# Moving the fourth weight unit's low part to GpSimd and the second residual tile to VectorE at the borders of a decoder trunk

## The chip, the cores and the metric

The kernel runs on one core of a Trainium2 chip. The metric is the device time of one execution in microseconds. A run is the time of one execution; the numbers below are the median of three runs, and one more execution that was profiled.

## The reference

The reference is a decoder trunk of four layers over 272 tokens (16 learned ones and 256 of the input) with 1024 features, in float32. Every layer has three sub-layers, and each is wrapped in two norms:

```
h = h + 0.5 * rmsnorm(swiglu_1(rmsnorm(h, g0)), g1)
h = h +       rmsnorm(mixer   (rmsnorm(h, g2)), g3)
h = h + 0.5 * rmsnorm(swiglu_2(rmsnorm(h, g4)), g5)
```

`rmsnorm(x, g)` is `x * rsqrt(mean(x*x) + eps) * g`. The mixers are stick-breaking attention (layers 0 and 3), latent attention with a rotary key (layer 1) and RWKV-7 time mixing (layer 2). A SwiGLU is `silu(h @ gate) * (h @ up)` times an output matrix, with 2816 hidden features.

## The kernel before

The activations lie with the features on the 128 partitions: `h`, `m`, `x_hi` and `x_lo` hold eight tiles of 128 features by 272 tokens each. A product in nearly full float32 precision is made of three passes of TensorE over numbers that are split in two: with `w = w_hi + w_lo` and `x = x_hi + x_lo` it adds `w_hi*x_hi`, `w_hi*x_lo` and `w_lo*x_hi` into one bank of PSUM.

The weights come in units of up to 1408 columns of 128 features, one after the other through a ring of four slots. SyncE loads a unit into `raw`, ScalarE copies it into `w_hi` (`split_hi`), and GpSimd subtracts `w_lo = raw - w_hi` in two halves (`split_lo`, line 1685). TensorE waits for `lo_ready` of a unit before it uses it, and SyncE waits for it before it loads the slot again. A run of units that belong to one matrix is a section. All engines have their own program, written out by hand in order, and they meet only at semaphores; the order of the work on an engine is the order of the code.

A **border** is the place where one sub-layer ends and the next begins. There are eleven of them inside the trunk, and what happens there is this:

- TensorE ends the output matrix, sums the squares of the output (lines 452 and 454) and runs some products that nobody reads (line 460).
- ScalarE makes the factor `rsqrt(mean + eps)` with two instructions (1193 and 1196) and writes it to bank 4 of PSUM.
- VectorE scales the eight tiles of the output, `m[k] = m[k] * gain * bank[4]` (line 1918, below "scale k"). Tile 0 it adds to the residual itself, `h[0] += m[0]` (line 1922). The call `steps.link` makes it wait for its own scale first.
- GpSimd adds the tiles 1 to 7, `h[k] += m[k]` (`add_residual`, line 1719), each as soon as VectorE has scaled it.
- ScalarE makes `x_hi[k] = h[k] * gain` (line 1227) as soon as tile k of `h` is there, and then its squares (1229).
- VectorE makes the low part `x_lo[k] = h[k] * gain - x_hi[k]` (line 1825, below "low k"). With `LAG = 3` low 0 stands behind scale 3 in its program, low 1 behind scale 4, and so on.
- TensorE begins the next section with `first_round` (line 384): for each tile k it waits for `x_hi[k]`, does the four products of the first two units that need only that (416 and 417), for odd k also three products of the third unit (400 to 402), then waits for `x_lo[k]` and does two more products (424). It goes to tile k + 1 only then. The next norm's own factor is not needed for this: it is applied to the results.
- Behind low 7 VectorE adds up the squares (1832 to 1834) for the sum that TensorE makes in line 382.

Three of the next section's first four units get their low part from GpSimd during the last round of the section before (`output_section`). The fourth one's is made by VectorE (line 1910), between the copy of the last output tile and scale 0. The border that leads to time mixing (its next section is called `lora1`) is apart: there GpSimd makes the fourth unit's low part behind the residual, in one instruction of 1024 columns. The border to latent attention uses the tiles through `product` (lines 339 to 341), which needs `x_hi` and `x_lo` at once.

Of the kernel before, what the change touches and what calls it, by code (L numbers as in the profile page):

```python
# [19 lines left out]
P = 128  # L20
D = 1024
DT_ = D // P
# [7 lines left out]
RING = 4  # L30
# [4 lines left out]
LAG = 3  # L35
SUM_AFTER = 6
FILL = 10
WARM = 12
NCH, LEVELS = 5, 6
PAIRS = 4  # L40
# [58 lines left out]
def build(nc, A, out, layers):  # L99
    secs = sections(plan_of(layers))  # L100
    ctx = ExitStack()
    with ctx:
# [4 lines left out]
        h = sb("h", [P, DT_, L])  # L107
        m = sb("m", [P, DT_, L])
        raw = sb("raw", [P, RING, CAP * P])
# [19 lines left out]
        bank = [ctx.enter_context(nc.psum_tensor(f"bank{b}", [P, 512], F32)) for b in range(8)]  # L129
# [3 lines left out]
        w_hi, w_lo = (xplace.enter_context(nc.sbuf_tensor(n, [P, RING, CAP * P], F32R)) for n in ("w_hi", "w_lo"))  # L133
# [89 lines left out]
        hi_ready, lo_ready = sem("hi_ready"), sem("lo_ready")  # L223
# [6 lines left out]
        apply_ready, h_ready = sem("apply_ready"), sem("h_ready")  # L230
# [31 lines left out]
        def rounds(eng, sec, body, ahead, peel=False):  # L262
# [6 lines left out]
                    body(i, lambda s: ahead(sec, i + 1, s))  # L269
            after = following[sec.name_key]  # L270
            body(sec.iters - 1, lambda s: ahead(after, 0, s) if after else None)

        def fourth_unit_by_vector(sec):

            return following[sec.name_key] is not None and following[sec.name_key].name != "lora1"

        def leads_to_mixing(sec):

            return following[sec.name_key] is not None and following[sec.name_key].name == "lora1"
# [10 lines left out]
        following = {s.name_key: t for s, t in zip(secs, secs[1:] + [None])}  # L290

        def gain(layer, sub, post, j):
            c = ((layer * 3 + sub) * 2 + post) * DT_ + j
            return gains[:, c:c + 1]
# [6 lines left out]
        def _(pe):  # L301
# [10 lines left out]
            def taken(*banks):  # L312
                for b in banks:
                    pe.wait_ge(bank_free[b], uses[b] + 1)
# [132 lines left out]
            def sum_output(after):  # L447
# [8 lines left out]
                if after is not None:  # L456
                    taken(7)
                    pe.wait_ge(cbf_ready, 1)
                    for _ in range(FILL):
                        nc.tensor.matmul(bank[7][:, :], ident_bf, cbf[:, 0:512], start=True, stop=True)  # L460
# [656 lines left out]
            taken(7)  # L1117
            for _ in range(WARM):
                nc.tensor.matmul(bank[7][:, 0:L], std[:, 0:P], std[:, :], start=True, stop=True)
# [554 lines left out]
        def _(pool):  # L1674
# [19 lines left out]
            def output_section():  # L1694


                sec = next(take)

                def body(i, ahead):
                    for s in range(RING):  # L1700
                        if not (following[sec.name_key] is not None and s == 3 and isinstance(i, int) and i == sec.iters - 1):
                            ahead(s)
                rounds(pool, sec, body, split_lo)
                if following[sec.name_key] is None:
                    for at, k in enumerate((1, 3, 5, 7)):
                        pool.wait_ge(apply_ready, n["apply"] + at + 1)
                        c = slice(n["cut"], L)
                        nc.gpsimd.tensor_tensor(h[:, k, c], h[:, k, c], m[:, k, c], ALU.add).then_inc(last_pool_ready, 1)
                else:
                    add_residual(sec)  # L1710
                if leads_to_mixing(sec):
                    split_lo(following[sec.name_key], 0, 3)

            def add_residual(sec):
                for k in range(1, DT_):
                    n["apply"] += 1
                    pool.wait_ge(apply_ready, n["apply"])
                    c = slice(n["cut"], L)
                    nc.gpsimd.tensor_tensor(h[:, k, c], h[:, k, c], m[:, k, c], ALU.add).then_inc(h_ready, 1)  # L1719
# [7 lines left out]
            def time_mixing():  # L1727
                for s in range(RING):
                    pool.wait_ge(lhi_ready, s + 1)
                    nc.gpsimd.tensor_tensor(lr_lo[:, s, :], lt[:, s, :], lr_hi[:, s, :], ALU.subtract).then_inc(lr_ready, 1)  # L1730
                for _ in range(5):
                    next(take)
                vec = lambda c: vecs[:, c:c + 1]

                def level_part(lv, p):

                    total = chunks_of(lv)
                    if lv > 1:
                        pool.wait_ge(y_done, core_at[("Y", lv - 1), p][3] + 2)
                    for s in (2 * p, 2 * p + 1):  # L1740
                        nc.gpsimd.tensor_tensor(chunks(aml[:, s, 0:TC * total]), chunks(am[:, s, 0:TC * total]), per_chunk(m_level[lv], total),
                                                ALU.mult).then_inc(aml_ready, 1)

                for p in range(PAIRS):
                    X, first, second, _ = core_at["A", p]
                    pool.wait_ge(bank_free[X], first + 1)
                    pool.wait_ge(bank_free[X + 1], second + 1)
                    pool.wait_ge(gram_done, core_at["Rb", p][3] + 2)
                    for s in (2 * p, 2 * p + 1):
                        nc.gpsimd.tensor_tensor(chunks(tinv[:, s, :]), chunks(am[:, s, :]), per_chunk(m_level[0], NCH),  # L1750
                                                ALU.mult).then_inc(level0_made, 1)
                    for s in (2 * p, 2 * p + 1):
                        pool.wait_ge(level0_made, s + 1)
                        nc.gpsimd.tensor_tensor(chunks(tinv[:, s, :]), chunks(tinv[:, s, :]), per_chunk(ident64, NCH),
                                                ALU.add).then_inc(tinv0_ready, 1)
                    level_part(1, p)
                    for k in (2 * p, 2 * p + 1):
                        pool.wait_ge(bank_free[k], uses_at["bonus"][k] + 2)
                        nc.gpsimd.tensor_scalar_add(m[:, k, :], m[:, k, :], vec(V_LNB + k)).then_inc(offset_made, 1)
                for lv in range(2, LEVELS):  # L1760
                    for p in range(PAIRS):
                        level_part(lv, p)
                for k in range(DT_):
                    pool.wait_ge(offset_made, k + 1)
                    nc.gpsimd.tensor_tensor(m[:, k, :], m[:, k, :], g_[:, k, :], ALU.mult).then_inc(offset_ready, 1)
                for k in range(DT_):
                    pool.wait_ge(offset_ready, k + 1)
                    nc.gpsimd.tensor_scalar_mul(g_[:, k, :], g_[:, k, :], vec(V_LNW + k)).then_inc(scaled_gate_ready, 1)
                pool.wait_ge(sa_done, 4 * NCH)
                sec_out = next(take)  # L1770
                for s in range(RING):
                    split_lo(sec_out, 0, s)
                low_parts(x_lo, x_hi, DT_)
                for s in range(RING):
                    split_lo(sec_out, 1, s)
                for s in range(3):
                    split_lo(following[sec_out.name_key], 0, s)
                add_residual(sec_out)

            pool.wait_ge(lo_ready, 2)  # L1780
# [29 lines left out]
        def _(dve):  # L1810
            steps = Steps(dve, dve_chain)
            n = dict(sq=0, sg=0, std=0, head=0, mhead=0, vt=0, xf=0, x=0, gained=0, hsq=0, kept=0, cut=0)
            cols = lambda: slice(n["cut"], L)
# [62 lines left out]
            def last_product(sec, layer, sub, then=None):  # L1876
# [25 lines left out]
                rounds(dve, sec, body, lambda *a: None)  # L1902
                n["sq"] += DT_
                n["kept"] += 1
                if fourth_unit_by_vector(sec):
                    after = following[sec.name_key]
                    w = slice(0, after.blocks * P)
                    dve.wait_ge(hi_ready, after.start + 4)
                    dve.wait_ge(lo_ready, after.start + 3)
                    nc.vector.tensor_tensor(w_lo[:, 3, w], raw[:, 3, w], w_hi[:, 3, w], ALU.subtract).then_inc(lo_ready, 1)  # L1910
                b = 2 if two else 3
                dve.wait_ge(bank_free[b], uses_at[sec.name_key][b] + sec.iters + 1)
                inverse_root()
# [1 line left out]
                    last_residual(layer, sub)  # L1915
                    return
                for k in range(DT_):
                    scaled = nc.vector.scalar_tensor_tensor(m[:, k, cols()], m[:, k, cols()], gain(layer, sub, 1, k), bank[4][:, cols()],  # L1918
                                                            ALU.mult, ALU.mult)
                    if k == 0:  # L1920
                        steps.link(scaled)
                        nc.vector.tensor_tensor(h[:, 0, cols()], h[:, 0, cols()], m[:, 0, cols()], ALU.add).then_inc(h_ready, 1)
                    else:
                        scaled.then_inc(apply_ready, 1)
                    if then and k >= LAG:
                        low_part(*then, k - LAG)
# [602 lines left out]
```

## Time and profile before

| | us |
|---|---|
| median of three runs | 2333.43 |
| lowest and highest | 2330.32, 2334.26 |
| the profiled execution | 2328.99 |
| its span, first to last instruction | 2327.2 |
| TensorE busy in the span | 2238.4 (96%) |
| GpSimd busy | 1701.5 (73%) |
| ScalarE busy | 1052.2 (45%) |
| VectorE busy | 906.4 (39%) |

The span is the time that the trace covers, and the profiled execution took 1.8 us more than it. A line of a timeline begins with the start of an instruction and how long it took, both in us; the brackets at its end tell how long the engine was idle before it, and what it then was released by. Matmuls overlap, so each is shown as longer than the distance to the next.

### The profile page before, as it was taken

What the parts mean: (1) busy time and instruction counts of PE and PEld (TensorE: products, weight loads), DVE (VectorE), ACT (ScalarE), POOL (GpSimd) and SP (SyncE); (2) the same over time, 40 slices, a digit from 0 to 9 for tenths busy, and PEclk for the clock granted to TensorE, in tenths of its full rate; (3) what the DMA queues carried; (4) which work ended last, traced back from release to release, by engine and by line L of the source; (5) the groups of instructions that cost most, each with busy time, mean ns of one, the idle gap of its engine ahead of it and who ended that gap; (6) DMA issues with size and microseconds to landing.
All of it is one profiled execution on the core that took longest, in us unless ns stands there. A gap on an engine that the chain in (4) does not pass through costs nothing. (4 is left out here: it accounts for less than half of the span.)

```text
span 2327.2 us, 54272 instructions
## 1 busy us (share of the span) xinstructions
PE 2238.4 (96%) x20693; PEld 2175.7 (93%) x20704; DVE 906.4 (39%) x1911; ACT 1052.2 (45%) x1545; POOL 1701.5 (73%) x1306
## 2 busy tenths in 40 slices
PE   9999999999999889999999898789999999999998
PEld 8999999999999879999999897679999999999997
DVE  4322334313331434322431987734322331344331
ACT  5444545444443545344444573335444434465442
POOL 6887758887887728887888403838887888766996
PEclk9999999999999999999999999999999999999999
DMA  6553544554554314563555242015554555433662
GB/s 217 171 196 126 158 127 152 173 199 128 179 192 146 127 46 154 171 199 127 181 185 180 99 157 68 3 39 163 174 197 134 172 179 188 141 126 127 191 206 99
DMA packets 90125, 348.82 MB, mean 150 GB/s; under 512 B 10016, under 2 KB 11808, under 8 KB 90016
## 3 DMA queue, kind: packets, MB, share of 16 engines
q1 hardware_dynamic: 90016, 347.31, 46.2%
q8 instruction: 75, 1.23, 0.2%
q14 instruction: 34, 0.28, 0.0%
HBM read 346.22 MB, written 1.05 MB: 149 GB/s over the span
## 5 line engine op out<-in xcount | busy, mean ns | idle before, releaser
L1685 POOL TENSOR_TENSOR w_lo<-raw,w_hi 128x512 fp32r<-128x512 f32 (+4 forms) x1124 | 1547.0, 1412 | 420.7 <-ACT w_hi L1182 401.2
L339 PE MATMUL bank<-x_hi,w_hi 128*128 128x272 f32 (+1 forms) x3264 | 946.3, 290 | 3.5 <-DVE x_lo L1825 1.9
L341 PE MATMUL bank<-x_hi,w_lo 128*128 128x272 f32 (+1 forms) x3264 | 942.2, 289 | 0.0
L340 PE MATMUL bank<-x_lo,w_hi 128*128 128x272 f32 (+1 forms) x3264 | 938.3, 287 | 0.0
L1182 ACT ACTIVATE w_hi<-raw 128x1024 fp32r<-128x1024 f32 (+2 forms) x608 | 678.7, 1119 | 386.4 <-PE bank L341 368.7
L339 PEld LDWEIGHTS bank<-x_hi,w_hi 128*128 128x128 f32 x3264 | 615.5, 189 | 7.0 <-DVE hid_lo L1963 3.1
L340 PEld LDWEIGHTS bank<-x_lo,w_hi 128*128 128x128 f32 x3264 | 616.1, 189 | 0.1
L341 PEld LDWEIGHTS bank<-x_hi,w_lo 128*128 128x128 f32 x3264 | 615.6, 189 | 0.0
L339 PE MATMUL bank<-hid_hi,w_hi 128*128 128x272 f32 (+1 forms) x1408 | 404.1, 287 | 0.0
L341 PE MATMUL bank<-hid_hi,w_lo 128*128 128x272 f32 (+1 forms) x1408 | 403.7, 287 | 0.0
L340 PE MATMUL bank<-hid_lo,w_hi 128*128 128x272 f32 (+1 forms) x1408 | 403.0, 286 | 0.0
L339 PEld LDWEIGHTS bank<-hid_hi,w_hi 128*128 128x128 f32 x1408 | 265.0, 188 | 0.0
L340 PEld LDWEIGHTS bank<-hid_lo,w_hi 128*128 128x128 f32 x1408 | 264.9, 188 | 0.0
L341 PEld LDWEIGHTS bank<-hid_hi,w_lo 128*128 128x128 f32 x1408 | 264.6, 188 | 0.0
L1286 ACT ACTIVATE sg<-gs 128x272 f32<-128x272 f32 (+1 forms) x176 | 75.6, 429 | 393.7 <-DVE gs L1844 393.7
L1895 DVE COPY m<-bank 128x272 f32 (+3 forms) x96 | 42.1, 439 | 523.1 <-ACT sq L1187 523.1
L1956 DVE TENSOR_TENSOR bank<-bank,xr 128x272 f32<-128x272 f32 (+1 forms) x176 | 78.6, 447 | 394.1 <-PE bank L341 394.1
L1187 ACT ACTIVATE sq<-bank 128x272 f32<-128x272 f32 (+1 forms) x96 | 38.0, 396 | 239.9 <-PE bank L341 233.1
L1844 DVE TENSOR_TENSOR gs<-bank,xr 128x272 f32<-128x272 f32 (+1 forms) x176 | 77.2, 439 | 161.7 <-PE bank L341 142.6
L1719 POOL TENSOR_TENSOR h<-h,m 128x272 f32<-128x272 f32 (+1 forms) x77 | 70.5, 949 | 40.0 <-DVE m L1918 40.0
L1961 DVE CAST hid_hi<-bank 128x272 f32 (+3 forms) x176 | 77.3, 439 | 24.6 <-DVE bank L1959 12.9
L1959 DVE TENSOR_TENSOR bank<-sg,bank 128x272 f32<-128x272 f32 (+1 forms) x176 | 78.1, 444 | 21.7 <-ACT sg L1286 16.2
(379 smaller groups left out, 2367.7 us busy)
## 6 DMA issues: line engine op xcount, KB each, us to landing
raw<-in_ffn_in SPq DMA_DIRECT2D x352, 512.0 KB, 3.5
raw<-in_ffn_out SPq DMA_DIRECT2D x128, 704.0 KB, 4.1
raw<-in_sb_in SPq DMA_DIRECT2D x48, 512.0 KB, 3.5
raw<-in_rw_in SPq DMA_DIRECT2D x24, 512.0 KB, 3.2
raw<-in_sb_out SPq DMA_DIRECT2D x16, 512.0 KB, 3.5
raw<-in_mla_out SPq DMA_DIRECT2D x8, 512.0 KB, 3.2
raw<-in_rw_lora SPq DMA_DIRECT2D x8, 512.0 KB, 3.2
raw<-in_rw_out SPq DMA_DIRECT2D x8, 512.0 KB, 4.0
```

What stands on the lines that cost most here:

```text
L339: nc.tensor.matmul(o, wh, xh[:, k, cols()], start=start, stop=False)
L340: nc.tensor.matmul(o, wh, xl[:, k, cols()], start=False, stop=False)
L341: last = nc.tensor.matmul(o, wl, xh[:, k, cols()], start=False, stop=stop)
L1182: nc.scalar.activation(w_hi[:, s, 0:sec.blocks * P], raw[:, s, 0:sec.blocks * P], ACT.Copy).then_inc(hi_ready, 1)
L1286: nc.scalar.activation(sg[:, f, cols()], gs[:, f, cols()], ACT.Silu).then_inc(sg_ready, 1)
L1685: part = nc.gpsimd.tensor_tensor(w_lo[:, s, w], raw[:, s, w], w_hi[:, s, w], ALU.subtract)
L1719: nc.gpsimd.tensor_tensor(h[:, k, c], h[:, k, c], m[:, k, c], ALU.add).then_inc(h_ready, 1)
L1844: last = nc.vector.tensor_tensor(dst, bank[b][:, cols()], xr[:, cols()], ALU.mult)
L1895: nc.vector.tensor_copy(m[:, per * i + t, cols()], bank[b][:, cols()]).then_inc(bank_free[b], 1)
L1956: nc.vector.tensor_tensor(up, up, xr[:, cols()], ALU.mult).then_inc(up_made, 1)
L1959: nc.vector.tensor_tensor(up, sg[:, f, cols()], up, ALU.mult).then_inc(hid_made, 1)
L1961: nc.vector.tensor_copy(hid_hi[:, 2 * i + f, cols()], up).then_inc(hhi_made, 1)
```

## The change

`BY_VECTOR = 2` says how many tiles VectorE adds to the residual. VectorE no longer makes the low part of the fourth unit; GpSimd makes it, in two halves like the others, before the residual (the border to time mixing keeps its own order). VectorE scales the tiles 0 and 1 into banks 6 and 5 of PSUM instead of into `m`, and adds both from there to `h`. GpSimd adds the tiles 2 to 7.

```
-        def fourth_unit_by_vector(sec):
-            return following[sec.name_key] is not None and following[sec.name_key].name != "lora1"
...
                 def body(i, ahead):
                     for s in range(RING):
-                        if not (following[sec.name_key] is not None and s == 3 and isinstance(i, int) and i == sec.iters - 1):
+                        if not (leads_to_mixing(sec) and s == 3 and isinstance(i, int) and i == sec.iters - 1):
                             ahead(s)
...
             def add_residual(sec):
-                for k in range(1, DT_):
+                for k in range(BY_VECTOR, DT_):
...
                 for s in range(RING):
                     split_lo(sec_out, 1, s)
-                for s in range(3):
+                for s in range(RING):
                     split_lo(following[sec_out.name_key], 0, s)
                 add_residual(sec_out)
...
-                if fourth_unit_by_vector(sec):
-                    after = following[sec.name_key]
-                    w = slice(0, after.blocks * P)
-                    dve.wait_ge(hi_ready, after.start + 4)
-                    dve.wait_ge(lo_ready, after.start + 3)
-                    nc.vector.tensor_tensor(w_lo[:, 3, w], raw[:, 3, w], w_hi[:, 3, w], ALU.subtract).then_inc(lo_ready, 1)
...
                 for k in range(DT_):
-                    scaled = nc.vector.scalar_tensor_tensor(m[:, k, cols()], m[:, k, cols()], gain(layer, sub, 1, k), bank[4][:, cols()],
+                    grown = bank[6 - k][:, cols()] if k < BY_VECTOR else m[:, k, cols()]
+                    scaled = nc.vector.scalar_tensor_tensor(grown, m[:, k, cols()], gain(layer, sub, 1, k), bank[4][:, cols()],
                                                             ALU.mult, ALU.mult)
-                    if k == 0:
+                    if k < BY_VECTOR:
                         steps.link(scaled)
-                        nc.vector.tensor_tensor(h[:, 0, cols()], h[:, 0, cols()], m[:, 0, cols()], ALU.add).then_inc(h_ready, 1)
+                        nc.vector.tensor_tensor(h[:, k, cols()], h[:, k, cols()], grown, ALU.add).then_inc(h_ready, 1)
```

The rows below are VectorE's program at the first border, from the copy of the last output tile to scale 4, before the change. Lines 1918 and 1922 are the scale and the add, 1825 is the low part of a tile.

```order
L1895 COPY m<-bank 128x272
L1910 TENSOR_TENSOR w_lo<-raw,w_hi 128x1024
L1918 SCALAR_TENSOR_TENSOR m<-m,gains,bank 128x272
L1922 TENSOR_TENSOR h<-h,m 128x272
L1918 SCALAR_TENSOR_TENSOR m<-m,gains,bank 128x272 x3
L1825 SCALAR_TENSOR_TENSOR x_lo<-h,gains,x_hi 128x272
L1918 SCALAR_TENSOR_TENSOR m<-m,gains,bank 128x272
```

The same place on VectorE in the changed kernel; its lines 1910, 1914 and 1822 are now the scale, the add and the low part.

```order
L1892 COPY m<-bank 128x272
L1910 SCALAR_TENSOR_TENSOR bank<-m,gains,bank 128x272
L1914 TENSOR_TENSOR h<-h,bank 128x272
L1910 SCALAR_TENSOR_TENSOR bank<-m,gains,bank 128x272
L1914 TENSOR_TENSOR h<-h,bank 128x272
L1910 SCALAR_TENSOR_TENSOR m<-m,gains,bank 128x272 x2
L1822 SCALAR_TENSOR_TENSOR x_lo<-h,gains,x_hi 128x272
L1910 SCALAR_TENSOR_TENSOR m<-m,gains,bank 128x272
```

The weight unit is gone from VectorE, and one more pair of scale and add stands ahead of low 0.

GpSimd's program at the first border before the change, from the last turn of the loop over the output matrix to the first round of the next section.

```order
L268 REGISTER_ALU
L268 COMPARE_AND_BRANCH
L1685 TENSOR_TENSOR w_lo<-raw,w_hi 128x512 x6
L1719 TENSOR_TENSOR h<-h,m 128x272 x7
L268 UNCONDITIONAL_BRANCH
```

The same place on GpSimd in the changed kernel (1682 is the low part of a weight unit, 1716 the add).

```order
L269 REGISTER_ALU
L269 COMPARE_AND_BRANCH
L1682 TENSOR_TENSOR w_lo<-raw,w_hi 128x512 x8
L1716 TENSOR_TENSOR h<-h,m 128x272 x6
L269 UNCONDITIONAL_BRANCH
```

GpSimd has two halves of a weight unit more ahead of the residual, and one tile of the residual less.

## Rows read from the trace of the kernel before

**Rows 1.** The page, busy time of each engine, share of the span, instructions.

```profile
PE 2238.4 (96%) x20693; PEld 2175.7 (93%) x20704; DVE 906.4 (39%) x1911; ACT 1052.2 (45%) x1545; POOL 1701.5 (73%) x1306
```

**Rows 2.** Waits of TensorE: us in total, times, longest.

```profile
PE bank L416 <- ACT x_hi L1227: 8.1, 9, 1.3
...
PE bank L424 <- DVE x_lo L1825: 2.3, 9, 0.3
```

**Rows 3.** Timeline of ScalarE at the first border: start, us, instruction, idle before.

```profile
215.45 0.40 ACT L1196 ACTIVATE bank<-std 128x272 f32<-128x272 f32 x1
```

**Rows 4.** Timeline of VectorE at the first border.

```profile
215.08 1.23 DVE L1910 TENSOR_TENSOR w_lo<-raw,w_hi 128x1024 fp32r<-128x1024 f32 x1 [0.50 <-ACT w_hi L1182]
216.22 0.49 DVE L1918 SCALAR_TENSOR_TENSOR m<-m,gains,bank 128x272 f32<-128x272 f32 x1
216.74 0.44 DVE L1922 TENSOR_TENSOR h<-h,m 128x272 f32<-128x272 f32 x1
217.10 1.31 DVE L1918 SCALAR_TENSOR_TENSOR m<-m,gains,bank 128x272 f32<-128x272 f32 x3
218.33 0.49 DVE L1825 SCALAR_TENSOR_TENSOR x_lo<-h,gains,x_hi 128x272 fp32r<-128x272 f32 x1
...
219.15 0.60 DVE L1825 SCALAR_TENSOR_TENSOR x_lo<-h,gains,x_hi 128x272 fp32r<-128x272 f32 x1
```

**Rows 5.** Timeline of GpSimd at the first border.

```profile
210.76 2.56 POOL L1685 TENSOR_TENSOR w_lo<-raw,w_hi 128x512 fp32r<-128x512 f32 x2 [1.37 <-ACT w_hi L1182]
217.67 0.77 POOL L1719 TENSOR_TENSOR h<-h,m 128x272 f32<-128x272 f32 x1 [4.36 <-DVE m L1918]
...
218.39 1.06 POOL L1719 TENSOR_TENSOR h<-h,m 128x272 f32<-128x272 f32 x1
```

**Rows 6.** Timeline of TensorE at the first border.

```profile
217.88 0.36 PE L416 MATMUL bank<-x_hi,w_hi 128*128 128x272 f32 x1 [0.85 <-ACT x_hi L1227]
218.08 0.29 PE L417 MATMUL bank<-x_hi,w_lo 128*128 128x272 f32 x1
218.21 0.29 PE L416 MATMUL bank<-x_hi,w_hi 128*128 128x272 f32 x1
...
218.88 0.51 PE L424 MATMUL bank<-x_lo,w_hi 128*128 128x272 f32 x2 [0.25 <-DVE x_lo L1825]
```

**Rows 7.** Timelines of ScalarE, VectorE and GpSimd at the border to time mixing.

```profile
1300.89 0.40 ACT L1196 ACTIVATE bank<-std 128x272 f32<-128x272 f32 x1
...
1301.40 0.50 DVE L1918 SCALAR_TENSOR_TENSOR m<-m,gains,bank 128x272 f32<-128x272 f32 x1 [1.92 <-ACT bank L1196]
...
1309.88 2.26 DVE L1825 SCALAR_TENSOR_TENSOR x_lo<-h,gains,x_hi 128x272 fp32r<-128x272 f32 x1 [0.29 <-ACT x_hi L1227]
...
1309.25 2.60 POOL L1685 TENSOR_TENSOR w_lo<-raw,w_hi 128x1024 fp32r<-128x1024 f32 x1
```

**Rows 8.** Forms and durations (ns, least, median, most) of the instruction of line 1959.

```profile
L1959 DVE TENSOR_TENSOR bank<-sg,bank x176: 428/446/447, 26.5 to 2253.5; 128x272 f32<-128x272 f32 x154, 128x256 f32<-128x256 f32 x22
```

**Rows 9.** Timelines of ScalarE and VectorE at the border behind time mixing.

```profile
1585.93 0.40 ACT L1196 ACTIVATE bank<-std 128x272 f32<-128x272 f32 x1
...
1587.18 0.49 DVE L1918 SCALAR_TENSOR_TENSOR m<-m,gains,bank 128x272 f32<-128x272 f32 x1
```

**Rows 10.** Timelines of VectorE, GpSimd and TensorE at the border to layer 3's attention.

```profile
2008.58 1.56 DVE L1834 TENSOR_TENSOR acc<-m 128x272 f32<-128x272 f32 x1
...
2008.55 2.71 POOL L1685 TENSOR_TENSOR w_lo<-raw,w_hi 128x512 fp32r<-128x512 f32 x2 [3.06 <-ACT w_hi L1182]
...
2010.19 0.50 PE L382 MATMUL bank<-acc,consts 128*128 128x272 f32 x1 [0.63 <-DVE acc L1834]
```

**Rows 11.** Border to latent attention: timeline of TensorE; busy times, clock (0.54) of 758 to 764.

```profile
757.54 0.36 PE L339 MATMUL bank<-x_hi,w_hi 128*128 128x272 f32 x1 [1.66 <-DVE x_lo L1825]
...
758.00:764.00 6.00, 5.78 (x21) 4.50 (x20) 5.13 (x11) 5.53 (x13) 4.64 (x6) 0.54 0.00 0
```

More of the change, by code:

```diff
@@ L37 @@
 FILL = 10
+BY_VECTOR = 2
 WARM = 12
```

## Prediction

> **What bounds the kernel now.** I read the busy times first, then TensorE's waits, then the timelines of the first border engine by engine, and last the same place at the other borders. TensorE is busy for 96% of the span [rows 1], so time is won or lost only where it waits. Of its waits two belong to the change, and each comes at nine borders: for the first high part of the activations, 8.1 us in all, and for the first low part, 2.3 us [rows 2]. The eleven borders are: eight of one pattern (the first shown; they start at 216, 345, 550, 886, 1091, 1792, 1998 and 2125 us), the one behind time mixing (1587), the one to time mixing (1301) and the one to latent attention (755).
>
> At the first border the reader is to see four clocks that run into each other. ScalarE has the norm's factor at 215.45 + 0.40 = 215.85 [rows 3]. VectorE scales tile 0 only at 216.22, since the fourth weight unit holds it from 215.08 for 1.23 [rows 4]. TensorE starts tile 0's four products at 217.88, is through with them at about 218.46 (they start 0.13 apart), and then stands until low 0, which ends at 218.33 + 0.49 = 218.82; it goes on at 218.88 [rows 4, 6]. After that it never stands again at this border. So what sets the end of the border is not the first high part but **low 0**: all that TensorE does behind 218.88 is in one piece, and a start of tile 0 that comes earlier only lengthens the wait behind it.
>
> **What the change does to low 0.** It is made up of four terms.
>
> The weight unit goes: at the border to time mixing, where VectorE has no unit to make, scale 0 starts at 1301.40, 0.11 behind the end of the factor (1300.89 + 0.40) [rows 7]. So here it would start at 215.96 in place of 216.22: -0.26. The 1.23 us of the instruction are not the gain, since it lay mostly beside the factor.
>
> The second pair comes in: scale to add is 0.52 start to start, add to the next scale 0.36, and scales follow each other by 0.41 (three in 1.31) [rows 4]. Before, low 0 stood 0.52 + 0.36 + 3 x 0.41 = 2.11 behind scale 0; now it is 2 x (0.52 + 0.36) + 2 x 0.41 = 2.58. That is +0.47. Both scales write to PSUM and both adds read from it, which no row of before shows for these two operations. The nearest is VectorE's product of the SwiGLU, which reads one operand from PSUM and writes there, 0.446 us [rows 8], against 0.44 for the add of now [rows 4]. From that alone I bound each of the four by -0.05 and +0.05, take 0, and keep +-0.2 a border.
>
> So low 0 would start at 215.96 + 2.58 = 218.54, against 218.33 now: +0.21.
>
> The third term is the one that I think decides. VectorE's low part reads two tiles of SBUF, GpSimd's add reads two as well, and the rows show that they take turns. Low 1 starts at 219.15 inside an add that runs from 218.39 to 219.45, and takes 0.60 in place of 0.49: it is held to 219.26, 0.19 before the add's end. That add itself takes 1.06 instead of 0.77, because low 0 was still reading when it began [rows 4, 5]. The clearest case is at the border to time mixing: a low part that starts at 1309.88 takes 2.26 us, because GpSimd began 2.60 us of weights at 1309.25 [rows 7]. An undisturbed add thus lets go 0.77 - 0.19 = 0.58 after its start. Today low 0 just escapes: GpSimd's first add starts at 217.67, lets go at 218.25, and low 0 starts at 218.33. In the changed kernel GpSimd's first tile is tile 2. Scale 2 starts at 215.96 + 2 x 0.88 = 217.72 and ends 0.49 later, and GpSimd starts 0.08 behind that (as 217.67 stands behind 217.10 + 0.49), at 218.29. Low 0 comes at 218.54, into the middle of it, is held to 218.29 + 0.58 = 218.87, and ends at 219.36 instead of 218.82: **+0.54** for low 0, and the same for TensorE. From there low parts and adds take turns every 0.94 us, as now, and TensorE needs 7.5 products of 0.125 = 0.94 per tile (six, and nine for every second), so it gets nothing back.
>
> The Trainium skill has this as a rule (SBUF — State Buffer, section "Who interferes with whom"): a VectorE instruction with two SBUF inputs and a GpSimd instruction that reads SBUF share a read interface, and the one that starts first keeps it for the whole instruction. By the rule word for word low 0 would be held to the add's end at 219.06 and end at 219.55, which gives +0.73 a border and 5.8 us in place of 4.5; the rows above, with a release 0.19 before the recorded end, give the smaller sum.
>
> The fourth term is the unit on GpSimd: two halves, 2.56 us together [rows 5], from about 215.1 (where VectorE took it up) to 217.7. GpSimd stands idle for 4.36 us there today [rows 5], and its first add is not due before 218.29. This costs nothing; the cover is 0.6 us. TensorE uses that unit's low part last of the four, so it is in time, and SyncE's next load of the slot, let go 1.4 us later, has the whole first round to land in. VectorE's scales and adds beside the two halves read one operand from SBUF and one from PSUM, as the instruction of line 1959 does, whose 447 ns at most show no holding beside a GpSimd that is 73% busy [rows 1, 8].
>
> **The sum over the borders.**
> - Seven of the pattern: 7 x 0.54 = +3.8.
> - The eighth, to layer 3's attention: +0.54 as well, but today TensorE stands 0.63 there for the sum of squares, because VectorE's last addition takes 1.56 behind a weight unit that GpSimd began at 2008.55 [rows 10]. In the changed kernel VectorE is about 0.3 earlier there (GpSimd has one add less) and the unit comes no earlier, so the addition slips ahead of it and the 0.63 go: -0.1.
> - Behind time mixing the factor is ready at 1586.33 and scale 0 starts only at 1587.18 [rows 9]; it gains 0.74, 0.48 more than elsewhere: +0.54 - 0.48 = +0.1.
> - To time mixing there was no weight unit on VectorE, so nothing is gained. The low parts come later by 0.47 and the wait, about 0.8, until the last two, and now two of them instead of one meet the 2.60 us of weights, since low 6 starts behind 1309.3. The last low part then ends some 0.35 later, and TensorE has nine products (1.1 us) between those two that used to lie in front. Between +0.35 and +1.1; I take +0.6.
> - To latent attention: the unit on VectorE has 768 columns there instead of 1024, so at most the 0.26 of the pattern is freed. TensorE takes the tiles as they come, waits 1.66 for the first, and has the half clock of 1.2 GHz behind that (0.54 granted from 758 to 764) [rows 11]. The low parts of tiles 0 to 5 come up to 0.8 later, the last not later, since GpSimd has one add less to make. Between -0.1 and +0.8; I take +0.2.
>
> Together 3.8 - 0.1 + 0.1 + 0.6 + 0.2 = **+4.6 us**. These come from an execution of 2328.99 (span 2327.2 and 1.8 around it), which would be 2333.6. It lay 4.4 below the median of the runs, 2333.43. I add to the median: **2338.0 us**, slower by 0.20%. No change is what lies within 0.2% or 4.7 us, about the least that a measurement of this kernel can tell; the forecast sits on that edge.
>
> **The rivals.**
>
> *The low part is not held.* If low 0 gets the read port beside GpSimd's add, the term is +0.21 instead of +0.54: 7 x 0.21 = 1.5, the eighth -0.4, behind time mixing -0.3, the other two 0.5 together: +1.3, 2334.7. For it: a low part's typical delay is only 0.1 us, and the port could be won by a few hundredths. Against it: every held row has GpSimd starting first, as it would here by 0.25 us.
>
> *Not slower.* The place is the chain of scale, add, scale, add. If results that stay in PSUM reach the next instruction sooner, so that the two pairs take 0.3 less, and low 0 is not held, then low 0 starts at or before 218.33; that is the point from which it decides. Then the seven borders cost nothing, the one behind time mixing gains 0.5 and the eighth 0.6: about -1.1, 2332.3. Against it: the rows have VectorE going from one instruction to the next at the same pace whether PSUM or SBUF is written.
>
> *TensorE's clock falls.* Today it stands 0.85 before tile 0 and 0.25 and a bit behind [rows 6]; in the changed kernel it would stand 0.6 and then about 1.05 (0.25 + 0.54 + 0.26). At the border to latent attention a wait of 1.66 and thin work behind it is followed by 6 us at half clock [rows 11]. One such stretch costs 3 us of work; at all eight borders 24, 2362. Against it: there TensorE waits for every tile, here for one.
>
> *The adds are held by the weight unit.* The change would then not do what it says: if VectorE's add out of PSUM waits for a half of the unit on GpSimd, the second add would stand until about 217.5 and low 0 moves by 1.5 a border, 8 x 1.5 = 12, 2346. The rows of line 1959 speak against it [rows 8].
>
> **How the numbers follow.** Forecast 0.55 (close to the edge: 0.43 of it slower, 0.56 no change, 0.01 faster), not held 0.19 (0.07, 0.88, 0.05), not slower 0.14 (0, 0.75, 0.25), clock 0.06 (0.9, 0.1, 0), held adds 0.06 (all slower). That gives slower 0.36, no change 0.59, faster 0.05. The forecast's own range is 2335 to 2341 (+-0.2 us at eight borders, and the bounds of the last two). The runs of one kernel spread over 4 us, so the range that also takes in "not held", part of "not slower" and the rule's longer hold, and leaves out the clock and the held adds, is 2331 to 2343.
>
> **What would show it.** In the changed profile: no weight unit on VectorE at a border and scale 0 about 0.1 behind the factor; low 0 with about 0.8 us instead of 0.49, begun inside GpSimd's first add; TensorE with a wait near 1 us ahead of the first low part at the eight borders; at layer 3's attention no wait for the sum; at the border to time mixing two long low parts or one of 2.6 us. A low 0 of 0.49 would break the third term; a scale into PSUM above 0.55 the second.

## The result, and the profile after

The changed kernel takes 2339.07 us, the median of ten runs (2335.63 to 2344.90); ten runs of the kernel before beside it give 2330.89 (2326.04 to 2334.26). The ratio is 1.0036 [1.0027, 1.0045]: slower by 0.36%, or 8.2 us at the medians. The forecast was 4.6 us, on its own edge between slower and no change, and it gave no change the larger chance (0.59 against 0.36). Its direction and its main mechanism hold. It went wrong in one term: it took nothing for TensorE's clock.

The profiled execution took 2339.09 us with a span of 2337.3, 10.1 longer than before. TensorE is busy 4.1 us longer with the same products, and the other 6.0 are waits.

The page of the changed kernel, busy time of each engine, beside [rows 1]:

```profile
PE 2242.5 (96%) x20704; PEld 2179.6 (93%) x20704; DVE 902.5 (39%) x1912; ACT 1051.8 (45%) x1545; POOL 1710.5 (73%) x1315
```

TensorE's waits in the changed kernel (us in total, times, longest), beside [rows 2]; 421 is now the first product that needs a low part, 413 the first that needs only a high part:

```profile
PE bank L421 <- DVE x_lo L1822: 9.4, 9, 1.1
...
PE bank L413 <- POOL w_lo L1682: 4.2, 7, 0.6
...
PE bank L413 <- ACT x_hi L1224: 1.2, 2, 0.6
```

The wait for low 0 grew from 2.3 to 9.4 us and the one for the high part fell from 8.1 to 4.2 + 1.2 = 5.4. Together that is +4.4 us at nine borders. Behind time mixing the two waits hardly changed (1.65 together, 1.59 before); at the other eight it is +0.54 each, as the prediction had it. The name "POOL w_lo" in the second line misleads: the wait is for several semaphores, and GpSimd's unit merely ended close to the high part. The code waits there for the low parts of the first two units and not for the fourth's.

The first border of the changed kernel, the engines one after the other (start, us, instruction, idle before), beside [rows 4 to 6]:

```profile
217.19 0.40 ACT L1193 ACTIVATE bank<-std 128x272 f32<-128x272 f32 x1
...
217.69 0.51 DVE L1910 SCALAR_TENSOR_TENSOR bank<-m,gains,bank 128x272 f32<-128x272 f32 x1 [1.38 <-ACT bank L1193]
218.23 0.44 DVE L1914 TENSOR_TENSOR h<-h,bank 128x272 f32<-128x272 f32 x1
218.59 0.50 DVE L1910 SCALAR_TENSOR_TENSOR bank<-m,gains,bank 128x272 f32<-128x272 f32 x1
219.12 0.44 DVE L1914 TENSOR_TENSOR h<-h,bank 128x272 f32<-128x272 f32 x1
219.48 0.90 DVE L1910 SCALAR_TENSOR_TENSOR m<-m,gains,bank 128x272 f32<-128x272 f32 x2
220.29 0.81 DVE L1822 SCALAR_TENSOR_TENSOR x_lo<-h,gains,x_hi 128x272 fp32r<-128x272 f32 x1
...
216.86 2.49 POOL L1682 TENSOR_TENSOR w_lo<-raw,w_hi 128x512 fp32r<-128x512 f32 x2 [1.80 <-ACT w_hi L1179]
220.05 0.76 POOL L1716 TENSOR_TENSOR h<-h,m 128x272 f32<-128x272 f32 x1 [0.70 <-DVE m L1910]
220.76 0.97 POOL L1716 TENSOR_TENSOR h<-h,m 128x272 f32<-128x272 f32 x1
...
219.37 0.36 PE L413 MATMUL bank<-x_hi,w_hi 128*128 128x272 f32 x1 [0.60 <-POOL w_lo L1682]
...
221.16 0.51 PE L421 MATMUL bank<-x_lo,w_hi 128*128 128x272 f32 x2 [1.05 <-DVE x_lo L1822]
```

The factor ends at 217.59 in place of 215.85; this 1.74 is older than the border (a stretch at half clock at the start of the program lies at 23.7 us in this execution, and at 11.0 in that of the kernel before) and comes off every row. Scale 0 starts 0.10 behind the factor. Low 0 starts at 220.29, inside GpSimd's first add, which began at 220.05, and takes 0.81 instead of 0.49; it ends at 221.10, and the prediction's 219.36 + 1.74 is 221.10. TensorE goes on at 221.16 after standing 0.60 and 1.05 close together, where it stood 0.85 and 0.25 before [rows 6].

What the prediction's sum has no term for is the next row. Busy times of the changed kernel (stretch, its length, then each engine, TensorE's granted clock, DMA share, GB/s) behind the first border, behind the second, and behind the one that follows time mixing:

```profile
221.60:225.00 3.40, 3.40 (x17) 3.40 (x16) 3.40 (x8) 3.06 (x9) 3.40 (x5) 0.51 0.25 100
225.00:228.40 3.40, 3.40 (x28) 3.40 (x28) 3.37 (x5) 1.23 (x4) 0.45 (x1) 0.99 0.01 2
352.00:356.00 4.00, 3.98 (x32) 3.98 (x32) 4.00 (x9) 3.64 (x10) 4.00 (x5) 1.00 0.29 112
1597.20:1600.60 3.40, 3.40 (x17) 3.40 (x17) 3.40 (x9) 3.06 (x8) 3.40 (x5) 0.50 0.34 130
```

From 221.6 to 225.0 the granted clock is 0.51, the lower level of 1.2 GHz, and only 17 matmuls are recorded in it against 28 in the next stretch of the same length. The same comes at 1597.2 and at 2010.2 us: behind three of the nine borders that begin with these products. Before, there was none behind any of them. Behind the second border, with the same waits, the clock stays at 1.00: the standing makes it likely, it does not decide it.

The whole span by places, from the distances between one border's sum of squares and the next (after less before):

| place (start before, us) | predicted | measured | of it half clock |
|---|---|---|---|
| 345, 550, 886, 2125 | +0.54 each | +0.53, 0.55, 0.54, 0.45 | 0 |
| 1091 and 1792 | +0.54 each | +0.91, 0.17 | 0 |
| 216 | +0.54 | +2.07 | 1.6 |
| 1587, behind time mixing | +0.1 | +1.60 | 1.5 |
| 1998, layer 3's attention | -0.1 | +0.81 | 1.3 |
| 755, latent attention | +0.2 | +0.80 | 0 |
| 1301, to time mixing | +0.6 | -0.08 | not to be told apart |
| start of the program | 0 | +1.74 | all, not of the change |

The price of a half-clock stretch is worked out from the run with the filled wait (below), which has the same path and no half clock behind these borders: its distances there are +0.51, +0.05 and -0.47, so the three stretches cost 1.56, 1.55 and 1.28. So this pair of executions is 4.0 us of path, 4.4 of clock behind borders, and 1.7 at the start. The last differs in the same way between kernels that have nothing to do with it: it is there in three of the experiments' profiles (+1.5 to +1.9) and not in the five others (-0.1 to +0.2), which all leave the start as it is. The four profiles that have it show the start's stretch at 23.2 to 23.7 us, the others at 11.0 to 12.0 or none. If the path is 4.0 in the runs too, about 4.2 of the 8.2 us of the medians are clock; that is a difference, not a measurement of its own.

### The profile page after: what moved, and what is told of

Read it like the earlier page. It is cut to its first block and busy times, and to the rows that moved or that the text cites. A ratio compares the mean times of both kernels' runs of the same rounds, so it can differ in the third digit from the quotient of the medians.

```text
span 2337.3 us, 54283 instructions
## 1 busy us (share of the span) xinstructions
PE 2242.5 (96%) x20704; PEld 2179.6 (93%) x20704; DVE 902.5 (39%) x1912; ACT 1051.8 (45%) x1545; POOL 1710.5 (73%) x1315
## 3 DMA queue, kind: packets, MB, share of 16 engines
HBM read 346.22 MB, written 1.05 MB: 149 GB/s over the span
## 5 line engine op out<-in xcount | busy, mean ns | idle before, releaser
L1682 POOL TENSOR_TENSOR w_lo<-raw,w_hi 128x512 fp32r<-128x512 f32 (+2 forms) x1144 | 1567.7, 1402 | 449.3 <-ACT w_hi L1179 428.9
L1955 DVE TENSOR_TENSOR hid_lo<-bank,hid_hi 128x272 f32 (+3 forms) x176 | 77.4, 440 | 20.2
```

The costliest lines, as they stand in the source:

```text
L1682: part = nc.gpsimd.tensor_tensor(w_lo[:, s, w], raw[:, s, w], w_hi[:, s, w], ALU.subtract)
L1955: nc.vector.tensor_tensor(hid_lo[:, 2 * i + f, cols()], up, hid_hi[:, 2 * i + f, cols()], ALU.subtract).then_inc(bank_free[2 * f + 1], 1)
```

## The experiments

The theory: low 0 is held by GpSimd's first add and ends 0.54 later (path), and TensorE's longer standing brings half clock behind some borders (clock). The first rival: GpSimd cannot take the fourth unit for nothing, and the unit is the cost. The second: results in PSUM reach the next instruction late, and the two scales and adds are the cost. "Clean borders" below are those at 216, 345, 550 and 886, as far as the profile in question shows no half clock behind them; their distances are against the kernel before.

**The unit alone.** The changed kernel, but VectorE adds one tile:

```diff
-BY_VECTOR = 2
+BY_VECTOR = 1
```

> The changed kernel with BY_VECTOR = 1: the fourth unit stays on GpSimd, tile 0 goes through PSUM, GpSimd adds tiles 1 to 7 again. Theory A (low 0 is held by GpSimd's first add, and TensorE's longer standing brings stretches of half clock): low 0 stands 2.11 us behind scale 0, GpSimd's first add lets go 0.08 before it, so low 0 takes 0.49, TensorE's wait ahead of it falls from 1.05 to 0.25, and no half clock follows a border. Scale 0 starts 0.26 earlier than in the kernel before at eight borders and 0.7 earlier behind time mixing: 2 to 3 us faster than the kernel before. Rival B (the two half units more on GpSimd are the cost): still about 8 us slower than before. Rival C (results kept in PSUM are the cost): half of it, about 4 us slower.

Measured: 2328.71 us against 2330.13, ratio 0.9993 [0.9983, 1.0002]; clean borders -0.15 to -0.18. Its second border, and behind it the one that follows time mixing:

```profile
346.65 0.55 DVE L1822 SCALAR_TENSOR_TENSOR x_lo<-h,gains,x_hi 128x272 fp32r<-128x272 f32 x1
...
343.68 2.49 POOL L1682 TENSOR_TENSOR w_lo<-raw,w_hi 128x512 fp32r<-128x512 f32 x2 [0.51 <-ACT w_hi L1179]
346.13 0.77 POOL L1716 TENSOR_TENSOR h<-h,m 128x272 f32<-128x272 f32 x1
...
347.25 0.52 PE L421 MATMUL bank<-x_lo,w_hi 128*128 128x272 f32 x2 [0.30 <-DVE x_lo L1822]
...
1585.80 2.19 POOL L1716 TENSOR_TENSOR h<-h,m 128x272 f32<-128x272 f32 x3
...
1586.05 2.24 DVE L1822 SCALAR_TENSOR_TENSOR x_lo<-h,gains,x_hi 128x272 fp32r<-128x272 f32 x1
...
1588.35 0.82 PE L421 MATMUL bank<-x_lo,w_hi 128*128 128x272 f32 x2 [2.00 <-DVE x_lo L1822]
```

The fourth unit lies on GpSimd as in the changed kernel, and at the clean borders nothing is lost. The gain there is a little less than the -0.26 of the weight unit, because the unit ends so late here that GpSimd goes straight on to its first add (no idle time in the row at 346.13), and low 0 runs into the end of that: 0.55 in place of 0.49. So the unit's cover, 0.6 us with two tiles on VectorE, is used up with one. Behind time mixing the unit does cost something: GpSimd's weights end so late that its first three adds follow one another without a gap, and low 0 is held through all three, 2.24 in place of 0.49. TensorE stands 2.00, half clock follows from 1587.7 to about 1594.5, and the distance there is +3.75. None of the other eight borders has half clock. So the expected 2 to 3 us did not come, and the 1.4 us at the medians can't be told from no change.

**Low 0 one scale earlier.** The changed kernel with

```diff
-LAG = 3
+LAG = 2
```

> The changed kernel with LAG = 2: low 0 stands behind scale 2 instead of scale 3. Theory A: low 0 starts 2.17 us behind scale 0, ahead of GpSimd's first add (2.33), takes 0.49 and ends 0.2 us earlier than in the kernel before; GpSimd's add is now the one that is held, by about 0.2. TensorE's wait ahead of low 0 is about 0.3 and no half clock follows a border: 1 to 2.5 us faster than the kernel before. Rivals B and C: nothing that they blame has changed, so still about 8 us slower than before.

Measured: 2329.07 us, ratio 0.9992 [0.9982, 1.0002]; clean borders -0.16 to -0.20. Its second border:

```profile
348.29 0.49 DVE L1822 SCALAR_TENSOR_TENSOR x_lo<-h,gains,x_hi 128x272 fp32r<-128x272 f32 x1
...
348.45 0.96 POOL L1716 TENSOR_TENSOR h<-h,m 128x272 f32<-128x272 f32 x1 [0.70 <-DVE m L1910]
...
348.84 0.52 PE L421 MATMUL bank<-x_lo,w_hi 128*128 128x272 f32 x2 [0.32 <-DVE x_lo L1822]
```

This is the case that separates best: all parts of the change are there, unit on GpSimd, two tiles through PSUM, and the loss is gone (by the times alone it can't be told from the kernel before). Low 0 now begins 0.16 ahead of GpSimd's add and takes its 0.49; the add pays with 0.96. The border comes out by the prediction's own terms: -0.26 + 0.47 - 0.41 (one scale less ahead of it) = -0.20. And TensorE, which stands 0.32 there in place of 1.04, keeps its clock at 1.00 behind all nine borders of this profile. Both rivals fall here: the unit and the PSUM results are still in it.

**TensorE at work while it waits.** The changed kernel with four products that nobody reads ahead of the wait for low 0:

```diff
+WAIT_FILL = 4
...
                     if behind_norm:
+                        if k == 0 and sec.start:
+                            for _ in range(WAIT_FILL):
+                                nc.tensor.matmul(bank[7][:, :], ident_bf, cbf[:, 0:512], start=True, stop=True)
                         pe.wait_ge(x_ready, base + k + 1)
```

> The changed kernel, with four products that nobody reads (0.22 us each) put on TensorE between tile 0's high parts and its wait for low 0. Theory A: low 0 still takes 0.8 us and TensorE goes on no sooner, but it does not stand, so no half clock follows a border: about 4 us slower than the kernel before instead of 8. If the clock has no part in the loss: still about 8 us slower. If the added products are in the way of the real ones: more than 8.

Measured: 2335.38 us, ratio 1.0025 [1.0015, 1.0034]; clean borders +0.51 to +0.57. Its first border and the busy times behind it:

```profile
218.56 0.81 DVE L1826 SCALAR_TENSOR_TENSOR x_lo<-h,gains,x_hi 128x272 fp32r<-128x272 f32 x1
...
219.42 0.52 PE L425 MATMUL bank<-x_lo,w_hi 128*128 128x272 f32 x2 [0.18 <-DVE x_lo L1826]
...
219.00:229.00 10.00, 9.82 (x77) 9.55 (x76) 8.23 (x15) 7.08 (x14) 5.96 (x7) 1.00 0.16 52
```

Low 0 is held as before (0.81), so the path is the same, but TensorE no longer stands for it and the clock stays at 1.00. There is no half clock behind any of the nine borders of this profile. That shows the cause in the trace: what the filled wait takes away at these borders is the clock's part alone. By the times it is less sharp: +5.3 against +8.2 us, and the intervals overlap by 0.07%. Latent attention and time mixing, which have half clock of their own, moved as well in this profile (-2.5 and +4.0 us), so its whole span says little about the path.

**The clock's part without the change.** The kernel before, with half of the unread products at the end of a section:

```diff
-FILL = 10
+FILL = 5
```

> The kernel before with FILL = 5 instead of 10: five of the products that nobody reads are left out, so TensorE stands about 1.9 us ahead of tile 0 instead of 0.85, and nothing that anyone waits for is later. If standing at a border is what brings the half clock: low 0 takes 0.49 and ends when it did, but stretches of half clock (3.4 us each, 1.6 to 1.7 us lost) appear behind borders, 2 to 8 us slower than before. If the half clock in the changed kernel came from something else: as fast as before.

Measured: 2337.32 us against 2329.84, ratio 1.0024 [1.0015, 1.0032]. Its first border:

```profile
217.81 0.36 PE L416 MATMUL bank<-x_hi,w_hi 128*128 128x272 f32 x1 [1.93 <-ACT x_hi L1227]
...
218.25 0.49 DVE L1825 SCALAR_TENSOR_TENSOR x_lo<-h,gains,x_hi 128x272 fp32r<-128x272 f32 x1
...
219.00:222.40 3.40, 3.40 (x16) 3.40 (x16) 3.40 (x8) 2.97 (x8) 3.40 (x5) 0.50 0.05 22
```

Here nothing on the path moved: low 0 is at its old place with 0.49. Only TensorE stands longer, 1.93 instead of 0.85, at the place where its unread products were. Half clock comes behind five of the nine borders; these cost 1.25 to 1.53 us each and the other four 0.0. So standing at a border is enough, without any of the change's parts.

**The tiles alone.** The kernel before with the two tiles through PSUM, and the fourth unit left on VectorE:

```diff
+BY_VECTOR = 2
...
-                for k in range(1, DT_):
+                for k in range(BY_VECTOR, DT_):
...
-                    scaled = nc.vector.scalar_tensor_tensor(m[:, k, cols()], ...
+                    grown = bank[6 - k][:, cols()] if k < BY_VECTOR else m[:, k, cols()]
+                    scaled = nc.vector.scalar_tensor_tensor(grown, ...
...
-                    if k == 0:
+                    if k < BY_VECTOR:
                         steps.link(scaled)
-                        nc.vector.tensor_tensor(h[:, 0, cols()], h[:, 0, cols()], m[:, 0, cols()], ALU.add).then_inc(h_ready, 1)
+                        nc.vector.tensor_tensor(h[:, k, cols()], h[:, k, cols()], grown, ALU.add).then_inc(h_ready, 1)
```

> The kernel before with only the second half of the change: tiles 0 and 1 scaled into PSUM and added by VectorE, the fourth unit still made by VectorE ahead of scale 0. Theory A (low 0 held by GpSimd's first add, then half clock): low 0 stands 2.58 us behind scale 0 instead of 2.11, is held to about 0.8 us, and since scale 0 is not freed it ends 0.8 us later than in the kernel before at eight borders: 6 us, and 4 to 6 more from half clock behind borders, 10 to 12 slower than before. Rival B (the fourth unit on GpSimd is the cost): as fast as before.

Measured: 2342.81 us against 2329.84, ratio 1.0049 [1.0036, 1.0062]; the clean border at 345 +0.82, the three others, which have half clock behind them, about 2.3. Its second border, and the stretch behind its first:

```profile
351.78 0.81 DVE L1826 SCALAR_TENSOR_TENSOR x_lo<-h,gains,x_hi 128x272 fp32r<-128x272 f32 x1
...
352.64 0.52 PE L425 MATMUL bank<-x_lo,w_hi 128*128 128x272 f32 x2 [1.04 <-DVE x_lo L1826]
...
221.50:224.90 3.40, 3.36 (x15) 3.36 (x16) 3.40 (x8) 3.10 (x8) 3.40 (x5) 0.50 0.00 0
```

The unit was not moved and the loss is larger, 0.82 against 0.53 at the border shown. The terms give 0.47 + 0.33 = 0.80, the second pair and the hold, without the 0.26 that the moved unit gives. The first rival falls a second time, and the terms add up. In all it is 13.0 us, a little more than the 10 to 12 expected, with half clock behind five of the nine borders.

**The two tiles through SBUF.** The changed kernel with

```diff
-                    grown = bank[6 - k][:, cols()] if k < BY_VECTOR else m[:, k, cols()]
+                    grown = m[:, k, cols()]
```

> The changed kernel with the scaled tiles 0 and 1 kept in m instead of PSUM, so that VectorE's two adds read two SBUF operands each while GpSimd makes the fourth unit's low part. If adds and weights take turns at one read port: the first add is held to the end of GpSimd's second half, 0.8 to 1.1 us long in place of 0.44, low 0 comes later by about as much, and the kernel is 8 to 10 us slower than the changed one (16 to 18 slower than before). Rival C (PSUM is the cost): as fast as the kernel before. If the place of the result doesn't matter: as slow as the changed kernel, about 8.

Measured: 2350.27 us, ratio 1.0085 [1.0071, 1.0099]; clean borders +1.5, that is 1.0 over the changed kernel. In all it is 20.1 us slower than before, more than the 16 to 18 expected, with half clock behind five of the nine borders. Its first border, and behind it all of the changed kernel's adds out of PSUM (ns, least, median, most):

```profile
216.65 1.42 DVE L1914 TENSOR_TENSOR h<-h,m 128x272 f32<-128x272 f32 x1
...
215.28 2.49 POOL L1682 TENSOR_TENSOR w_lo<-raw,w_hi 128x512 fp32r<-128x512 f32 x2 [1.81 <-ACT w_hi L1179]
...
218.76 0.36 PE L413 MATMUL bank<-x_hi,w_hi 128*128 128x272 f32 x1 [1.57 <-ACT x_hi L1224]
```

```profile
L1914 DVE TENSOR_TENSOR h<-h,bank x22: 420/436/439, 218.2 to 2135.4; 128x272 f32<-128x272 f32 x20, 128x256 f32<-128x256 f32 x2
```

With both operands in SBUF the first add stands behind GpSimd's weights and takes 1.42 us. With one of them in PSUM, 22 adds take 0.44 at the most, in the same place beside the same weights. The Trainium skill says this (SBUF — State Buffer, section "Who interferes with whom": an instruction of VectorE with at most one SBUF input does not contend with GpSimd, if it is in none of the modes that use both port pairs), and the trace agrees. The second rival falls: PSUM is what keeps the change from being much worse.

**A version from the experiments.** The fourth unit is shared, so that VectorE's half lies in its idle time ahead of the factor and GpSimd's half ends early; one tile on VectorE; low 0 behind scale 2. `shares_unit` holds at every border but the one to time mixing, and GpSimd's list ahead of the residual goes back to three whole units. Against the changed kernel:

```diff
-LAG = 3
+LAG = 2
-BY_VECTOR = 2
+BY_VECTOR = 1
...
             def add_residual(sec):
+                if shares_unit(sec):
+                    n["half"] += 1
+                    pool.wait_ge(half_ready, n["half"])
+                    w = slice(0, (following[sec.name_key].blocks + 1) // 2 * P)
+                    nc.gpsimd.tensor_tensor(w_lo[:, 3, w], raw[:, 3, w], w_hi[:, 3, w], ALU.subtract).then_inc(lo_ready, 1)
...
+                if shares_unit(sec):
+                    after = following[sec.name_key]
+                    w = slice((after.blocks + 1) // 2 * P, after.blocks * P)
+                    dve.wait_ge(hi_ready, after.start + 4)
+                    nc.vector.tensor_tensor(w_lo[:, 3, w], raw[:, 3, w], w_hi[:, 3, w], ALU.subtract).then_inc(half_ready, 1)
```

> A version drawn from the theory: BY_VECTOR = 1 with tile 0 through PSUM, the fourth unit shared (VectorE makes its second half while ScalarE makes the factor, GpSimd the first half behind that), LAG = 2. Theory A: scale 0 is freed (0.26 earlier), GpSimd is free again before its first add, low 0 stands behind scale 2 and is held there by 0.3 but still ends 0.3 us earlier than in the kernel before at eight borders and 0.8 behind time mixing; TensorE stands less. 3 us faster than the kernel before, 2327. If the shared half delays scale 0 or GpSimd's first add: no faster.

Measured: 2327.16 us against 2329.84, ratio 0.9983 [0.9973, 0.9994]; clean borders -0.32 to -0.35. Its second border:

```profile
343.47 0.69 DVE L1916 TENSOR_TENSOR w_lo<-raw,w_hi 128x512 fp32r<-128x512 f32 x1 [0.50 <-ACT w_hi L1184]
344.36 0.51 DVE L1925 SCALAR_TENSOR_TENSOR bank<-m,gains,bank 128x272 f32<-128x272 f32 x1 [0.20 <-ACT bank L1198]
...
346.07 0.82 DVE L1832 SCALAR_TENSOR_TENSOR x_lo<-h,gains,x_hi 128x272 fp32r<-128x272 f32 x1
...
345.83 0.77 POOL L1726 TENSOR_TENSOR h<-h,m 128x272 f32<-128x272 f32 x1 [0.32 <-DVE m L1925]
...
346.95 0.51 PE L426 MATMUL bank<-x_lo,w_hi 128*128 128x272 f32 x2 [0.18 <-DVE x_lo L1832]
```

It is faster than both kernels. VectorE's half is through 0.20 ahead of scale 0, so it holds nothing up. Low 0 stands one scale earlier, but so does GpSimd's first add, at 345.83, and low 0 is held again (0.82): -0.26 - 0.41 + 0.33 = -0.34 a border.

The same with `LAG = 3`, where low 0 should come behind that add:

> The same with LAG = 3. Theory A: GpSimd's first add, no longer behind its weights, lets go just ahead of low 0, which takes 0.49 and ends 0.25 us earlier than in the kernel before: 2 to 3 us faster than the kernel before.

Measured: 2327.02 us, ratio 0.9986 [0.9975, 0.9996]; clean borders -0.24 to -0.27, the weight unit alone. Low 0's place is worth 0.1 a border there, less than the two times can tell.

## Why the prediction was right, and where it failed

1. *The weight unit goes, -0.26.* Right. Scale 0 starts 0.10 behind the factor, and the version with `LAG = 3` gains 0.24 to 0.27.
2. *The second pair, +0.47, PSUM at no cost.* Right. Low 0 stands 220.29 - 217.69 = 2.60 behind scale 0, predicted 2.58; the scale into PSUM takes 0.50 to 0.51 and the add 0.44. That answers the rivals "not slower" and "held adds".
3. *Low 0 is held, +0.54 in all.* Right to a hundredth. It is shown three ways: with the hold gone by an earlier low 0, with one tile and almost no hold, and with the unit's gain taken out. The rival "not held" is wrong. The shorter hold was the right one: low 0 reads from 221.10 - 0.49 = 220.61, 0.20 before the recorded end of GpSimd's add (220.81). A hold over the whole add would have cost 0.19 more a border. (Beside that rule the prediction sets 4.5 us; eight borders at 0.54 are 4.3. Nothing else goes by it.)
4. *The fourth unit on GpSimd costs nothing.* Right with two tiles on VectorE: 0.70 of idle time are left behind it at the first border. With one tile the cover is gone: 0.06 shows at most borders, and 1.75 behind time mixing (2.24 in place of 0.49).
5. *The other borders.* Behind time mixing came out as predicted but for the clock. At layer 3's attention the wait for the sum went as predicted:

```profile
2017.04 0.44 DVE L1831 TENSOR_TENSOR acc<-m 128x272 f32<-128x272 f32 x1
...
2019.99 0.62 PE L379 MATMUL bank<-acc,consts 128*128 128x272 f32 x2
```

The addition takes 0.44 where it took 1.56, and TensorE's product has no idle time ahead of it, 0.63 before [rows 10]. Without the clock, in the run with the filled wait, the border gained 0.47 rather than 0.1; the rest is not explained, and 0.36, about as much, wanders between the borders at 1091 and 1792 too. At latent attention the loss was 0.80, the upper bound in place of the 0.2 taken: TensorE's first wait there grew from 1.66 to 2.46 [rows 11], and nothing came back behind it. It is the second pair and the hold, 0.47 + 0.33: the moved unit freed nothing there, since in the run with one tile that wait is 1.67. At the border to time mixing the low part was held as predicted:

```profile
1316.56 2.62 DVE L1822 SCALAR_TENSOR_TENSOR x_lo<-h,gains,x_hi 128x272 fp32r<-128x272 f32 x1
...
1316.30 2.57 POOL L1682 TENSOR_TENSOR w_lo<-raw,w_hi 128x1024 fp32r<-128x1024 f32 x1
...
1319.23 0.40 PE L764 MATMUL bank<-x_lo,w_hi 128*128 128x272 f32 x1 [1.29 <-DVE x_lo L1822]
```

One low part of 2.62 us, and 1.29 of waiting behind it. What that costs in the end can't be read: the distance over time mixing moves by -1.8 to +4.0 us between the kernels with its own stretches of half clock.

**The step that failed** is the sum, which took nothing for TensorE's clock. The path without the clock is 4.0 us in the profiled pair against the 4.6 predicted; the 4.4 beside it are stretches at half clock behind borders. The prediction had the mechanism as a rival, with the right waits (0.6 and 1.05, as measured), but gave it 0.06, because TensorE waits for only one tile at these borders. Its prices failed as well. A stretch costs 1.3 to 1.6 us, not the 3 that the six microseconds at latent attention suggested. And it was weighed as something that comes at all eight borders or not at all; it came at three of nine here.

**What was luck.** That 2338.0 lies only 1.1 us from the measured 2339.07, inside a range that left the clock out, is in part luck. The forecast was added to a median of three runs, 2333.43; the ten runs beside the changed kernel gave 2330.89, 2.5 lower. That made up for most of the 3.6 by which the slowdown was forecast too small. With 4.4 for the clock and the path as measured, the old base would have given 2341.8 and the median of the ten runs 2339.3.

**What stays open.** Why one border falls to the half clock and the next with the same waits does not. How much of the 8.2 us is clock by times alone: 2.9 from the median of the run with the filled wait, 4.2 from the difference to the path. And the cost at the border to time mixing.

## What to carry to other kernels

When an instruction on one engine is moved by a few tenths, look at which instruction of the neighbour begins just ahead of it: low 0 lost 0.33 us because the other engine's add came 0.24 earlier, and was free of it again one place further up in its program. Look also at how late the neighbour is: if its instructions have queued up, the hold can last through several of them. Where TensorE already stands close to its limit at a section's border, a longer standing has two prices, the wait itself and a chance of half clock behind it; put the second into the sum as stretches times their price, not as a rival of all or nothing. A result that only the next instruction needs goes well through PSUM, if the other reader of SBUF is GpSimd.

## What the runs showed of the hardware that was not expected

- Two waits of 0.60 and 1.05 us with four products between them brought a stretch of 3.4 us at a granted clock of 0.51 behind three of nine borders, and one wait of 1.93 behind five of nine; 0.85 and 0.25 brought none in the profile of the kernel before.
- Four unread products in the wait of 1.05 went with a granted clock of 1.00 behind all nine borders of that profile.
- Three of GpSimd's adds without a gap between them, 1585.80 to 1587.99, held VectorE's low part of 1586.05 through all three (2.24 us), in the run with one tile.
- VectorE's instruction with two operands in SBUF goes on 0.19 to 0.20 before the recorded end of the GpSimd add that holds it: at the first border of the changed kernel, and at the second border of the one with one tile, where low 0 of 0.55 ended at 347.20 and the add of 346.13 at 346.90.
